# Token gather in three segments, a mixer's end in token chunks, and experts' outputs combined from two rounded parts

## What is computed

```python
def gated_deltanet(...):                      # 4 heads of 128, half of a mixer
    o = chunk_gated_delta_rule(q, k, v, g, beta)
    o = rms_norm(o, norm_g) * jax.nn.silu(z)
...
    y = concatenate([y_gdn, y_nsa], axis=-1) @ w_out        # token_mix, 1024 x 1024
    x = x + mod[:, 1, 2][:, None, :] * y
...
def hier_moe(h, w_grp, b_grp, w_rt, b_rt, w_up, w_down):    # 32 experts, each token goes to 2
    gate = softmax(e_val) * g_gate
    expert = (g_idx * 8 + e_idx).reshape(-1)
    order = argsort(expert)                   # 544 token copies, sorted by expert
    ...
        a, u = split(xb @ w_up[e], 2)         # 1024 x 1024
        y = (silu(a) * u) @ w_down[e]         # 512 x 1024
    y = y[dest] * w_sorted[:, None]
    return zeros.at[tok].add(y)
```

## Time and profile before

| | |
|---|---|
| median of 3 runs | 2919.0 us (2915.11 to 2919.03) |
| the profiled execution | 2915.67 us |
| its span in the profile | 2913.9 us |
| PE busy | 2689.0 us (92%) |
| DVE busy | 1461.7 us (50%) |
| ACT busy | 776.3 us (27%) |
| first expert layer's loop, from its first up product | 1677.8 to 2158.1 |
| second expert layer's loop | 2426.6 to 2908.8 |
| mixers' ends, from the last chunk's output to the last output product | 495.4 to 522.8 and 1179.3 to 1206.1 |

### The profile page before, as it was taken

One profiled execution on the slowest core, in us unless ns is written; L12 is line 12 of the kernel. 1 busy time (PEld: TensorE's weight loads), 2 busy tenths in 40 slices (PEclk: granted clock), 3 DMA queues, 4 the chain that ended last, 5 costly groups with the idle time before them and its releaser, 6 DMA issues. The chain is left out here.

```text
span 2913.9 us, 45820 instructions
## 1 busy us (share of the span) xinstructions
PE 2689.0 (92%) x18838; PEld 1921.8 (66%) x18838; DVE 1461.7 (50%) x3312; ACT 776.3 (27%) x1476; POOL 0.2 (0%) x4
## 2 busy tenths in 40 slices
PE   5999897999999998899999999999989999999998
PEld 4998776899899777799777743333346784333333
DVE  4885774687786475575233423333332633333333
ACT  4332253333433153433233211111112331111110
POOL 0000000000000000000000000000000000000000
PEclk9999898999999898999999999999999999999999
DMA  7776420576576420265321289999972135999997
GB/s 302 277 272 233 158 74 2 203 289 255 194 274 260 147 102 31 87 246 194 110 73 58 88 324 427 427 427 428 428 308 87 59 145 220 415 427 427 428 427 297
DMA packets 72025, 701.58 MB, mean 241 GB/s; under 512 B 8704, under 2 KB 11136, under 8 KB 11392
## 3 DMA queue, kind: packets, MB, share of 16 engines
q1 hardware_dynamic: 71808, 698.54, 60.0%
HBM read 697.46 MB, written 1.05 MB: 240 GB/s over the span
## 5 line engine op out<-in xcount | busy, mean ns | idle before, releaser
L1528 PE MATMUL ps<-arena_parts 128*128 128x256 f32 x2112 | 603.7, 286 | 24.1 <-DVE arena_parts L3218 24.1
L1530 PE MATMUL ps<-arena_parts,ring_parts 128*128 128x256 f32 x2112 | 600.6, 284 | 0.0
L1529 PE MATMUL ps<-arena_parts 128*128 128x256 f32 x2112 | 598.6, 283 | 0.0
L1300 PE MATMUL ps<-ring,arena 128*64 128x512 f32 x2048 | 467.1, 598 | 0.3 <-DMA ring<-slabs 0.3
L1528 PEld LDWEIGHTS ps<-arena_parts 128*128 128x128 f32 x2112 | 402.5, 191 | 25.5 <-issue 25.3
L1530 PEld LDWEIGHTS ps<-arena_parts,ring_parts 128*128 128x128 f32 x2112 | 410.5, 194 | 0.0
L1529 PEld LDWEIGHTS ps<-arena_parts 128*128 128x128 f32 x2112 | 402.9, 191 | 0.2
L833 PE MATMUL ps<-h,ring 128*128 128x256 f32 (+1 forms) x1536 | 375.3, 404 | 19.4 <-DVE h L2561 10.0
L833 PEld LDWEIGHTS ps<-h,ring 128*128 128x128 f32 x1536 | 303.0, 200 | 74.5 <-issue 10.9
L3132 DVE TENSOR_TENSOR ring_parts<-ring,arena_parts 128x2048 fp32r<-128x2048 f32 x132 | 299.4, 2289 | 74.1 <-ACT arena_parts L1690 74.1
L1690 ACT CAST arena_parts<-ring 128x2048 fp32r<-128x2048 f32 x132 | 249.6, 1904 | 317.4 <-DMA ring<-slabs 310.3
(11 more groups left out here) (409 smaller groups left out, 2477.5 us busy)
## 6 DMA issues: line engine op xcount, KB each, us to landing
ring<-slabs SPq DMA_DIRECT2D x190, 2048.0 KB, 14.6
ring<-slabs SPq DMA_DIRECT2D x278, 1024.0 KB, 5.0
sq<-aside SPq DMA_DIRECT2D x2, 1024.0 KB, 8.5
arena<-aside SPq DMA_DIRECT2D x2, 1024.0 KB, 10.5
x<-xT SPq DMA_DIRECT2D x1, 1024.0 KB, 8.7
outT<-x SPq DMA_DIRECT2D x1, 1024.0 KB, 4.6
constants<-const SPq DMA_DIRECT2D x1, 1004.5 KB, 6.3
vectors<-vec SPq DMA_DIRECT2D x1, 747.5 KB, 4.3
```

What stands on the lines that cost most here:

```text
L1300: mm = nc.tensor.matmul(ps[W * hh:W * hh + W, e % 2, :], xe[:, e % 2, 4 * k + c], wt[:, c], start=(k == 0 and c == 0), stop=(k == 1 and c ...
L1528: nc.tensor.matmul(out, w_hi, v_hi, start=start, stop=False, skip_group_check=True)
L1529: nc.tensor.matmul(out, w_hi, v_lo, start=False, stop=False, skip_group_check=True)
L1530: return nc.tensor.matmul(out, w_lo, v_hi, start=False, stop=stop, skip_group_check=True)
```

## The change

**Gather.** The 544 slots are cut in three segments, 0 to 128, 128 to 272 and 272 to 544. Only the first is gathered ahead of the loop. Expert 0 gathers the whole second one, experts 1 and 2 four width slabs of the third each. The second `keep_clock` has 2 matmuls instead of 5. ACT takes the copies for experts 2 and 3 later.

**Combine.** `YSB` is replaced by two rounded parts of the output times its gate: ACT writes `y_hi` with a scale per partition, DVE writes `y_lo` (`low_y`, a new operation per expert). The gate per slot comes out of `gate_rows` (accumulated, plus one small add), and `GE` becomes a 0/1 matrix, which costs DVE one more operation. A combine is 16 fp32r products. From expert 4 on `combine(e-1)` stands ahead of `down_part(e)`, not behind it.

**Mixer's end.** The norm is done by chunk (two operations of half the width for each one), and so is the product: a new kind of job, `first` (128 tokens, PSUM banks 7 and 5), and `out` for the second 128.

The core of the diff:

```diff
-PIECES = (range(0, 3), range(3, 6), range(6, KC))
+SEGMENTS = ((0, P), (P, T2), (T2, SLOTS))
+PIECES = ((1, range(KC)), (2, range(0, 4)), (2, range(4, KC)))
...
+        out += [(kind, c, 16 + c // 2, c % 2 * P, "dve") for kind in ("half", "first", "out") for c in range(KC)]
...
+                    elif st[0] == "mix" and kind in ("first", "out"):
+                        at, o = (0, ps[:, (7, 5)[idx % 2], 0:P]) if kind == "first" else (P, bank(b, P))
+                        if idx == 0:
+                            await_("dve", q, "y_gdn", at // P)
+                            await_("dve", q, "att", 1)
+                        for k in range(4):
+                            mm = nc.tensor.matmul(o, wt[:, k, c0:c0 + P], rhs[:, k, at:at + P], start=(k == 0), stop=(k == 3))
...
+                root_sums(0)
                 await_("act", q, "vn", 1)
...
                 mark(mm, q, "o", 1)
-                await_("act", q, "osq")
...
+                run_jobs(q, st, 53, 56, slab, job)
+                root_sums(1)
+                run_jobs(q, st, 56, 61, slab, job)
...
                 def combine(e):
...
+                    await2("dve", "ylo", e)
                     await2("dve", "ge", e)
...
-                            mm = nc.tensor.matmul(ps[:, 4 + 2 * (i % 2) + dh, 0:T2], ysb[rows64, e % 2, i * P:(i + 1) * P],
-                                                  ge[rows64, e % 2], start=True, stop=True)
+                            for y in (y_hi, y_lo):
+                                mm = nc.tensor.matmul(ps[:, 4 + 2 * (i % 2) + dh, 0:T2], y[rows64, e % 2, i * P:(i + 1) * P],
+                                                      ge[rows64, e % 2], start=y is y_hi, stop=y is y_lo)
...
-                keep_clock(2, 5)
+                keep_clock(2, 2)
...
+                    if e > 3:
+                        combine(e - 1)
                     down_part(e)
-                    if e:
+                    if 0 < e <= 3:
                         combine(e - 1)
...
-                    mark2(nc.scalar.copy(ysb[:, e % 2], ps[:, 3, :]), "ysb", e)
+                    await2("dve", "gslot", e)
+                    mark2(nc.scalar.activation(y_hi[:, e % 2], ps[:, 3, :], ACT.Copy, scale=view(GSLOT, 2, 3)[:, e % 2, 2:3]),
+                          "ysb", e)
...
+                for t in range(2):
+                    ts = slice(t * P, (t + 1) * P)
...
+                    for c in {0: range(3), 1: range(3, KC)}[t]:
+                        dve.wait_ge(s["proj_done"], job + 53 + c + 1)
...
+                def low_y(e):
+
+                    await2("act", "ysb", e)
+                    if e >= 2:
+                        await2("pe", "add", e - 2, 3)
+                    mark2(nc.vector.scalar_tensor_tensor(out=y_lo[:, e % 2], in0=ps[:, 3, :], scalar=gates2[:, e % 2, 2:3],
+                                                         in1=y_hi[:, e % 2].bitcast(F32), op0=ALU.mult, op1=ALU.subtract),
+                          "ylo", e)
...
+                    low_y(e)
                 add(NE - 1)
```

More of the change, by code:

```diff
@@ L460, in build @@
         h = sb("h", [P, KC, T2])
-        sq = sb("sq", [P, KC, T2])
+        sq, sq_parts = twice("sq", [P, KC, T2])
         hid = sb("hid", [P, 2, 2, T2])
@@ L686, in build @@
         most_at = view(INTS, NE + 1).bitcast(I32)[0:1, NE:NE + 1]
+        y_hi, y_lo = (sq_parts.rearrange("p k n -> p (k n)")[:, 1024 * a:1024 * a + 1024].rearrange("p (a n) -> p a n", a=2)
+                      for a in range(2))
         def expert_at(e):
@@ L778, in run_jobs @@
                         seen = sl
-                    back = 2 if kind == "half" else turns
+                    back = 2 if kind == "half" or (st[0], kind) == ("mix", "first") else turns
                     if (st[0], kind) == ("fox", "out") and idx == 0:
@@ L900, in gdn, with root_sums @@
             def gdn(q, l, st, slab, job):
+                def root_sums(t):
+                    await_("act", q, "osq", t)
+                    for c in range(GH):
+                        mm = nc.tensor.matmul(ps[:, t, c * P:(c + 1) * P], ones, sq[:, c, t * P:(t + 1) * P], start=True,
+                                              stop=True)
+                    mark(mm, q, "on", t)
                 qo = view(QO, 12, T1)
@@ L1261, in gather @@
                 hi, lo, pm = part(HTOK, 3, D), part(HTLO, 3, D), part(PM, 3, SLOTS)
+                lo_slot, end = SEGMENTS[half]
                 for t in range(3):
@@ L1269, in gather @@
                         for w, rows_of in enumerate((hi, lo)):
-                            mm = nc.tensor.matmul(bank(banks[(k - ks[0]) % 4], T2), rows_of[0:size, t, k * P:(k + 1) * P],
-                                                  pm[0:size, t, half * T2:(half + 1) * T2], start=(t == 0 and w == 0),
-                                                  stop=(t == 2 and w == 1))
+                            mm = nc.tensor.matmul(bank(banks[(k - ks[0]) % 4], end - lo_slot),
+                                                  rows_of[0:size, t, k * P:(k + 1) * P], pm[0:size, t, lo_slot:end],
+                                                  start=(t == 0 and w == 0), stop=(t == 2 and w == 1))
                     mark_at(mm, q, "xs", half, k)
@@ L1287, in sparse_pe @@
                 xe, hte, hide = view(XE, 2, KC, W), view(HTE, 2, 2 * P), view(HIDE, 2, 2, P)
-                ysb, ge = view(YSB, 2, 512), view(GE, 2, T2)
+                ge = part(GE, 2, T2)
                 def up_part(e, k):
@@ L1314, in down_part @@
                     if e:
-                        await2("act", "ysb", e - 1)
+                        await2("dve", "ylo", e - 1)
                     for hh in range(2):
@@ L1625, in _ @@
                     gdn(q, st[1], st, slab, job)
-                    await_("dve", q, "y_gdn")
-                    run_jobs(q, st, 53, 61, slab, job, behind=True)
+                    run_jobs(q, st, 61, 69, slab, job, behind=True)
                     slab += 20
@@ L2038, in take_sorted @@
                     wait_at("pe", q, "xs", half, k)
-                    if half == 1 and k == 0:
+                    if half == 2 and k == 0:
                         await_("dve", q, "xpad")
-                    mark_at(nc.scalar.copy(xs[:, k, half * T2:(half + 1) * T2], bank(banks[(k - ks[0]) % 4], T2)), q, "xs", half, k)
+                    lo_slot, end = SEGMENTS[half]
+                    mark_at(nc.scalar.copy(xs[:, k, lo_slot:end], bank(banks[(k - ks[0]) % 4], end - lo_slot)),
+                            q, "xs", half, k)
             def sparse_act(q, l):
                 mark2, await2 = stepper("act", l)
-                sile, ysb = view(SILE, 2, 2 * P), view(YSB, 2, 512)
+                sile = view(SILE, 2, 2 * P)
                 def gather(e):
@@ L2871, in place @@
             def place(q, half):
-                io = cst("iota", half * T2, T2)
+                lo_slot, end = SEGMENTS[half]
+                io = cst("iota", lo_slot, end - lo_slot)
                 for t, (at, size) in enumerate(KT2):
                     slot = view(SLOT, 3, 2)[0:size, t]
-                    pm = part(PM, 3, SLOTS)[0:size, t, half * T2:(half + 1) * T2]
+                    pm = part(PM, 3, SLOTS)[0:size, t, lo_slot:end]
                     mark(nc.vector.tensor_scalar(pm, io[0:size], slot[:, 0:1], None, ALU.is_equal), q, "p2", half, t)
@@ L2928, in sort_tokens @@
                 place(q, 1)
+                place(q, 2)
                 mark(nc.vector.memset(view(XS, KC, SLOTS + W)[:, :, SLOTS:], 0.0), q, "xpad")
```

94 lines of the change are left out of this document (52 added, 42 removed).

## The result

| | before | after |
|---|---|---|
| median | 2918.7 us (4 runs, 2915.1 to 2919.0) | 2938.8 us (4 runs, 2937.9 to 2945.3) |
| ratio | 1 | 1.0085 (1.0072 to 1.0097) |
| span in the profile | 2913.9 us | 2936.1 us |

The changed kernel is slower by 20 us in the medians and by 22.2 in the two profiles. The forecast was 30 more.

A forecast was written before the change was run, and what follows sets the result against it. Loads bound the expert layers' steady part, so only chain and tail count. Per layer 5.9 us without the clock plus 12.5 for it make 18.4, +37 for both; with -7 for the mixers, 2915.7 becomes 2946 us, range 2916 to 2958.

The forecast's parts named there:

- The bound: Expert layers: loads bound the steady part, so only microseconds in the chain before it or the tail behind count.
- First gather: Ahead of each expert loop: 128 columns instead of 272, .95 us a slab, 7.6 us, so -1.5 us.
- the gather inside the loop: Expert 0: an added 144-column segment of eight slabs at .97 us repeats 48 weight loads, +7.8 us.
- The rival by columns: First and expert 0's gathers: cost goes by columns, about 0 a layer, 2907 to 2911 us in all; chance .08.
- Clock keeping: Behind the first gather: six of ten records go, 6 x .256, so -1.5 us.
- Combines ahead of expert 3: Two early combines a layer: only the last step of each gets shorter, by .4 us, so -.8 us.
- The clock in the gathers: First gather to ups, and expert 0's gather with downs: clock falls to half, +4.3 and +5.7 us a layer.
- The tail: Behind each expert layer's last load: exposed combine and output parts cost +1.9 us, the clock +2.5 more.
- the clock's term: In the tail: two more sparse waits let the clock fall, +2.5 us (bounds 0 and +3.6).
- The mixers' ends: Last chunk's output to last product: -4.3 and -3.7 us, less 1 for the clock, so -7 (bounds -9 and 0).
- The sum: Whole kernel: +37 us for both expert layers and -7 for the mixers on 2915.7, giving 2946 us.

The follow-up runs named there:

- The test with wide gathers: Changed kernel with its two narrow gathers widened to 256 and 272 columns, no more weight loads; 1.0072 (1.0044 to 1.0101) to the kernel before.

## Why the prediction was right, point by point

**The bound.** Right. What a layer's chain and tail lost came out at its end, to within .7 us, and 20 us less of busy PE in the steady part gave nothing.

**First gather and the gather inside the loop.** Right to the hundredth where the clock is up: a slab is .95 to .96 us with 128 columns and .97 with 144 (start to start of six matmuls), and 1.13 with 272. The rival by columns (.6 and less) fell with that. The .27 us for the row changes I had only guessed; that the sum came out says nothing of the reason that I gave for it (shorter matmuls draining sooner), which no run tests. The Trainium skill ("TensorE: Matmul & The Clock Gate", section "Wait — 56ns, not 53.3ns?") gives 56 ns for 128 columns back to back. That isn't reached here, where each matmul has its weight load: inside a slab the closest two starts are .11 us apart.

**Clock keeping.** The size was right (-1.7 from gather to ups, forecast -1.5), the mechanism not: six records less would have been worth less, had PE's pause of 1.54 us not gone under the slow matmuls, and what sets the start is now ACT's copy, 2.3 us behind the gather. I had costed the change on PE alone and not asked what else the first ups wait for.

**Combines ahead of expert 3.** Right: 3.04 to 2.63 us, twice.

**The clock in the gathers.** Right in kind and place, a little large: in the second layer the first fall costs 9.49 - 7.6 = 1.9 us in the gather and 8.91 - 7.09 = 1.8 in the ups (3.7, forecast 4.3), the second 2.2 in the gather and 2.5 in the downs (4.7, forecast 5.7). In the first layer the kernel before had a fall of its own in the clock keeping (4.25 us for the ten records that took 2.56 in the second), which I left out of the sum: that is 1.7 of the difference there. In all the chains came to +10.7 and +12.1 where the forecast was +14.0 each. The test with wide gathers shows that the falls come with the narrow columns. The Trainium skill ("TensorE: Matmul & The Clock Gate", section "Part 1: The HAM clock gate (the "warmup" mystery)"), read as a rule on idleness, would have kept the clock: these gathers run without a gap (5.00 of 5.00 us busy) ahead of the fall, so the measurement decides against that reading.

**The tail.** Right in its course, step by step: wait for the low part, wait for the adds, the downs at half clock, wait again. From the last ups to the last add it is 23.7 and 24.3 us (20.0 and 21.4 before), +3.7 and +3.0, forecast +4.4. Of it the clock takes 2.85 us in the second layer (6.20 - 3.65 in the downs and .3 in the combine), 1.15 more than before's 1.7; in the first, which had no fall there before, 2.2. That leaves 1.8 and 1.5 for the exposed parts, where I had 1.9. So the clock's term was the one too large: 1.15 and 2.2 for 2.5.

**The mixers' ends.** Their course was right, with the wait behind out product 3 at 2.45 us (forecast 3.0), and the sum too: -3.4 and -4.4 us in the profiles (forecast -7 in all). In the time the gain is +1 to -13 us, -7.7 in the mean, so the forecast's -7 is right only as a mean over three places, and two of them lie beyond its bound of -9. What I didn't foresee is that 16 or 32 matmuls in front move a program by 7 to 17 us, as much as this gain or more.

**The sum.** By parts: 24.2 for the gather alone, 7.3 for the combine, -7.7 for the mixers make 23.8, beside 24.8 by the ratio. That they agree so well is luck in part, since the gather comes out at 16, 21 or 24 us and the whole change at 17 or 25, by the pair that one takes. The forecast for the same three was 29.6, 7.2 and -7. The 8 us between 30 and the profiles' 22.2 are 5.2 in the two chains, 2.1 in the tails and .8 in the mixers.

## What to carry to other kernels

A narrower matmul with a full weight load saves little (.95 for 1.13 us a slab, at less than half the columns), and a split that repeats weight loads pays them in full; if the clock then falls, the narrow form is slower than the wide one. Work that is moved ahead or cut up in a part bound by loads brings nothing, while the part's first and last microseconds count whole. For a change worth less than half a percent of a long program, time each version with a few instructions more in front, at several counts, before believing either sign.

## What the runs showed of the hardware that I had not expected

PE pauses 1 to 2 us in dense runs of 32 x 32 products, at times behind a block of 16 KB of instructions; the pauses of one program sum to 6 to 15 us in these kernels. 64 or 128 instructions more at the start move them (10.6 to 10.4 and 13.8 us) and the time (1 to .9990 and 1.0013), and with the mixers' change also what the clock costs (107 to 98 and 100 us, by the estimate above). That the pauses are waits for those blocks rests on the traffic beside them and on their moving with the program's length; the wait itself has no row. The pause of 1.1 to 1.6 us ahead of the clock keeping, where PE also reads a register and branches, may have another cause; that wasn't tried. The other surprise: the same stage shows its falls of the clock at other places in other kernels, so that two single profiles differ by several us in stages that the change doesn't touch (from the first expert layer's last add to the second's routing, -2.9 us from before to after).
